# Odd layer: the next tile's projection between the score products and the probability turns of each attention block

## The reference

```python
def sliding_window_attention(h, w_qkv, q_gain, k_gain, sinks):
    qkv = jnp.einsum('bld,de->ble', h, w_qkv)        # 1024 -> 1024 q + 128 k + 128 v
    ...
    q = rms_norm(q, q_gain) * (HEAD_DIM ** -0.5)     # 16 query heads of 64
    k = rms_norm(k, k_gain)                          # 2 key heads
    ...
    s = jnp.einsum('bnqhgd,bnkhd->bhgnqk', qb, kw)   # 128 queries x (128 before + 128 own) keys
    ...
    s = s - slopes * dist.astype(f32)
    s = jnp.where(valid, s, -jnp.inf)
    m = jnp.maximum(jnp.max(s, axis=-1, keepdims=True), sink)
    p = jnp.exp(s - m)
    p = p / (jnp.sum(p, axis=-1, keepdims=True) + jnp.exp(sink - m))
    o = jnp.einsum('bhgnqk,bnkhd->bnqhgd', p, vw)
```

## Time and profile before

| | |
|---|---|
| median of 3 runs | 974.62 us (974.48 to 975.08) |
| profiled execution | 972.04 us |
| its span | 970.3 us, so 1.74 us lie around it |
| mean granted TensorE clock | 0.915 of full speed |
| busy in the span | PE 812.2 us, DVE 588.8, ACT 471.8, POOL 180.3 |

### The profile page before, as it was taken

How to read it: one execution, slowest core, us unless ns; L and a number is a source line. 1 busy time by engine, 2 the same in 40 slices (tenths; PEclk the granted TensorE clock), 3 DMA queues, 4 the chain that set the end, 5 groups by cost and what they waited for, 6 DMA issues and landing times. The chain is left out here.

```text
span 970.3 us, 10750 instructions
## 1 busy us (share of the span) xinstructions
PE 812.2 (84%) x4088; PEld 578.6 (60%) x4088; DVE 588.8 (61%) x782; ACT 471.8 (49%) x640; POOL 180.3 (19%) x175
## 2 busy tenths in 40 slices
PE   4999999757799489998973999477779939999894
PEld 3455454357488468887751555344448827888673
DVE  2898842097734669988750322766613457898882
ACT  6052002431623258887754100577742517887872
POOL 5300002230001214333220000311100212333311
PEclk9999999959899589999995999588889959999998
DMA  9212012100522859999983005200033376999972
GB/s 378 106 53 88 31 57 87 44 1 1 227 98 104 310 205 327 327 330 316 334 281 113 1 0 173 88 1 1 1 129 110 136 288 242 328 333 337 304 253 35
DMA packets 31161, 159.53 MB, mean 164 GB/s; under 512 B 7680, under 2 KB 7808, under 8 KB 15744
## 3 DMA queue, kind: packets, MB, share of 16 engines
q1 hardware_dynamic: 17856, 127.93, 35.5%
q0 software_dynamic: 11520, 25.20, 9.2%
q10 hardware_dynamic: 1728, 5.64, 1.5%
HBM read 150.34 MB, written 25.17 MB: 181 GB/s over the span
## 5 line engine op out<-in xcount | busy, mean ns | idle before, releaser
L840 DVE TENSOR_TENSOR w_lo<-ring,w_hi 128x2048 fp32r<-128x2048 f32 x93 | 211.6, 2288 | 55.3 <-ACT w_hi L605 30.1
L1781 PE MATMUL PS<-w_hi,left_hi 128*128 128x512 f32 x512 | 177.1, 408 | 8.7 <-DVE left_hi L840 8.5
L605 ACT ACTIVATE w_hi<-ring 128x2048 fp32r<-128x2048 f32 x86 | 164.0, 1914 | 22.5 <-DMA ring<-stream 21.8
L1781 PEld LDWEIGHTS PS<-w_hi,left_hi 128*128 128x128 f32 x512 | 97.8, 191 | 31.1 <-DVE left_hi L840 11.7
L1781 PE MATMUL PS<-w_lo,left_hi 128*128 128x512 f32 x256 | 101.2, 395 | 0.0
L1805 PE MATMUL PS<-w_hi,left_lo 128*128 128x512 f32 x256 | 84.8, 392 | 5.0 <-DVE left_lo L840 3.3
L1870 PE MATMUL PS<-ring,hT 128*128 128x512 f32 (+1 forms) x192 | 71.6, 533 | 0.8 <-DVE hT L840 0.8
L475 POOL DMA_INDIRECT arena<-rows x32 | 50.9, 1591 | 82.4 <-PE PS L1763 65.6
L1805 PEld LDWEIGHTS PS<-w_hi,left_lo 128*128 128x128 f32 x256 | 48.0, 188 | 17.1 <-DVE left_lo L840 3.7
L1870 PEld LDWEIGHTS PS<-ring,hT 128*128 128x128 f32 x192 | 37.0, 194 | 34.5 <-issue 31.9
L660 ACT ACTIVATE arena<-PS 128x512 f32<-128x512 f32 x16 | 9.5, 596 | 97.1 <-PE PS L1521 97.1
(11 more groups left out here) (259 smaller groups left out, 1381.9 us busy)
## 6 DMA issues: line engine op xcount, KB each, us to landing
ring<-stream SPq DMA_DIRECT2D x110, 1024.0 KB, 12.4
arena<-stream SPq DMA_DIRECT2D x6, 1024.0 KB, 8.5
rows<-arena POOLq DMA_DIRECT2D x8, 512.0 KB, 3.2
x<-stream SPq DMA_DIRECT2D x4, 1024.0 KB, 5.8
x<-x_in SPq DMA_DIRECT2D x4, 512.0 KB, 5.4
sums<-x POOLq DMA_DIRECT2D x4, 512.0 KB, 4.1
x<-sums ACTq DMA_DIRECT2D x4, 512.0 KB, 5.2
out<-x POOLq DMA_DIRECT2D x4, 512.0 KB, 4.1
```

What stands on the lines that cost most here:

```text
L605: act.activation(w_hi[pair], held_slot(layer, m), ACT.Copy).then_inc(w_hi_done, 1)
L840: return V.tensor_tensor(out, a, b, op)
L1781: ins = mm(PS[:, 2, :], a, b, start=k == 0 and t == 0, stop=k == KD - 1 and t == 2)
```

## The change

TensorE's order in this stretch becomes one loop over tiles. Projections 1 to 3 are cut into pieces: a projection function takes the part and the rows of products, and the pieces go between the steps of the previous tile's attention. Scores use banks 0 and 1 for both halves, all projections banks 2 to 4, the turns of heads and probabilities banks 5 and 6, the product with the values bank 7. The queries' heads have two buffers instead of four. ACT and DVE get queues in matching order: heads of tile tt + 1 after the maximum of the second block of tile tt on DVE; squares, roots and exponentials alternating on ACT; all copies of heads on DVE; the first weight split straight after the first tile's root. On DVE an odd block's first bias stands ahead of the sums of the block before. The instructions' number and shapes in projection, scores, turns and products stay as they are. The core of the diff, in the order ACT, DVE, TensorE:

```diff
-        qn = cut(xs_t, 0, TT, QW)
+        qn = [arena[:, 21504 + QW * i:21504 + QW * (i + 1)] for i in range(2)]
...
+            act.wait_ge(at_zero, 1)
+            squares(0)
+            head_deviation(0)
+            weights_hi(1, 0)
+            exps(0)
+            normed_odd(0)
+            for u in range(8):
+                tt = u // 2 + 1
+                if u % 2 == 0 and tt < TT:
+                    squares(tt)
+                turned_probs(u)
+                if u % 2 == 0 and tt < TT:
+                    head_deviation(tt)
+                if u < 7:
+                    exps(u + 1)
+                attended_hi(u)
+                if u < 7:
+                    normed_odd(u + 1)
...
+            def biased(u, t):
+
                 pr = probs[u % 2]
-                if u >= 2:
+                if u >= 2 and t == 0:
                     dve.wait_ge(pt_psum, 4 * (u - 1))
...
+                dve.wait_ge(s_psum, 2 * u + t + 1)
+                for j in (2 * t, 2 * t + 1):
+                    for kv in range(2):
+                        head = 8 * kv + 4 * (u % 2) + j
+                        ins = stt(pr[:, 2 * j + kv, :], table, con("slope")[:, head:head + 1],
+                                  PS[:, kv, (j % 2) * 256:(j % 2) * 256 + 256], ALU.mult, ALU.add)
+                ins.then_inc(s_biased, 1)
...
+            normed_heads(0)
             for u in range(8):
-                biased(u)
-                summed(u)
-                if u >= 1:
-                    attended(u - 1)
+                tt = u // 2
+                if u % 2 == 0:
+                    if u:
+                        summed(u - 1)
+                    heads_out(tt)
+                    if u:
+                        attended(u - 2)
+                    biased(u, 0)
+                else:
+                    biased(u, 0)
+                    summed(u - 1)
+                    if u >= 2:
+                        attended(u - 2)
+                biased(u, 1)
+                most(u)
+                if u % 2 and tt + 1 < TT:
+                    normed_heads(tt + 1)
+            summed(7)
+            attended(6)
             attended(7)
...
+            def project(tt, part, ks):
+
+                if part == 0 and 0 in ks:
+                    pe.wait_ge(hT_done, 2 * TT + 2 * tt + 2)
+                    if tt:
+                        pe.wait_ge(qkn_done, tt)
+                n = 512 if part < 2 else 256
...
+            def turn_heads(tt):
+
+                pe.wait_ge(qkn_done, tt + 1)
+                if tt:
+                    pe.wait_ge(pt_done, 4 * (2 * tt - 1))
...
+            def att_scores(u, t):
+
                 n, jq = u // 2, u % 2
...
+                if t == 0 and jq == 0:
+                    pe.wait_ge(qT_done, 3 * n + 3)
+                if u + t:
+                    pe.wait_ge(s_biased, 2 * u + t)
...
+            def attend(u):
+
                 n = u // 2
-                if u + 1 < 8:
-                    att_scores(u + 1)
+                if u % 2 and n + 1 < TT:
+                    pe.wait_ge(qT_done, 3 * n + 6)
...
+            whole, low, high = range(KD), range(4), range(4, KD)
+            for part in range(3):
+                project(0, part, whole)
+            for t in range(1, TT):
+                turn_tile(1, t)
+            pe.wait_ge(hT_done, 4 * TT)
+            for tt in range(TT):
+                more = tt + 1 < TT
+                if more:
+                    project(tt + 1, 0, low)
+                turn_heads(tt)
+                if tt:
+                    attend(2 * tt - 1)
+                att_scores(2 * tt, 0)
+                if more:
+                    project(tt + 1, 0, high)
+                att_scores(2 * tt, 1)
+                if more:
+                    project(tt + 1, 1, whole)
+                    project(tt + 1, 2, whole)
+                att_scores(2 * tt + 1, 0)
+                att_scores(2 * tt + 1, 1)
+                attend(2 * tt)
+            attend(7)
```

More of the change, by code:

```diff
@@ L314, in if_over @@
                 body(over[layer])
[L316 to L324, removed]
         def k512(i):
@@ L789, in _, with squares @@
             norm(2)
-            act.wait_ge(at_zero, 1)
-            for tt in range(TT):
+            def squares(tt):
                 act.wait_ge(qkv_psum, tt + 1)
@@ L795, in _, with head_deviation, exps @@
                     act.wait_ge(ss_a, tt)
[L796 to L800, removed]
+                act.activation(sq1, PS[:, 2:4, :].rearrange("p a b -> p (a b)"), ACT.Square)
+                act.activation(arena[:, 1024:1152], PS[:, 4, 0:128], ACT.Square).then_inc(sqa_done, 1)
+                act.activation(vpad[:, 1 + tt, 0, 0:64], PS[:, 4, 128:192], ACT.Copy)
+                act.activation(vpad[:, 1 + tt, 1, 64:128], PS[:, 4, 192:256], ACT.Copy)
+            def head_deviation(tt):
                 act.wait_ge(ss_a, tt + 1)
                 act.activation(qstd, qss, ACT.Sqrt, bias=eps_t, scale=1.0 / HD).then_inc(qstd_s, 1)
[L803 to L806, removed]
+            def exps(u):
                 pr = probs[u % 2]
@@ L1373, in _, with normed_heads @@
             ts(kq_gain, par("q_gain"), HD ** -0.5, ALU.mult)
-            for tt in range(TT):
-                if tt in (1, 2):
-                    heads_out(tt - 1, (0, 1, 0), V.tensor_copy, dve)
-                b = 2 + 3 * (tt % 2)
+            def normed_heads(tt):
                 dve.wait_ge(sqa_done, tt + 1)
@@ L1857, in _ @@
             turn_tile(1, 0)
-            def project(tt):
-                pe.wait_ge(hT_done, 2 * TT + 2 * tt + 2)
-                b = 2 + 3 * (tt % 2)
-                if tt >= 2:
-                    pe.wait_ge(qkn_done, tt - 1)
-                for part in range(3):
-                    n = 512 if part < 2 else 256
-                    for k in range(KD):
-                        if tt == 0 and (k == 0 or k == 4 and part < 2):
-                            full(QKV0 + 2 * part + k // 4)
-                        w = k512(QKV0 + 2 * part + k // 4)[:, k % 4, :] if part < 2 else \
-                            slot(QKV0 + 4).rearrange("p (k n) -> p k n", n=256)[:, k, :]
-                        ins = mm(PS[:, b + part, 0:n], hT[:, k, tt * 128:tt * 128 + 128], w, start=k == 0, stop=k == KD - 1)
-                        if tt == 3 and part < 2 and k % 4 == 3:
-                            ins.then_inc(slot_free, 1)
-                ins.then_inc(qkv_psum, 1)
@@ L1875, in turn_heads @@
-            def turn_heads(tt, banks):
-                pe.wait_ge(qkn_done, max(tt + 1, 4) if tt >= 2 else tt + 1)
+            def project(tt, part, ks):
[4 more added lines that the diff above has]
+                n = 512 if part < 2 else 256
+                for k in ks:
+                    if tt == 0 and (k == 0 or k == 4 and part < 2):
+                        full(QKV0 + 2 * part + k // 4)
+                    w = k512(QKV0 + 2 * part + k // 4)[:, k % 4, :] if part < 2 else \
+                        slot(QKV0 + 4).rearrange("p (k n) -> p k n", n=256)[:, k, :]
+                    ins = mm(PS[:, 2 + part, 0:n], hT[:, k, tt * 128:tt * 128 + 128], w, start=k == 0, stop=k == KD - 1)
+                    if tt == 3 and part < 2 and k % 4 == 3:
+                        ins.then_inc(slot_free, 1)
+                if part == 2:
+                    ins.then_inc(qkv_psum, 1)
+                    pending[0] = 1 if tt == 3 else 0
```

97 lines of the change are left out of this document (36 added, 61 removed).

## The result

The changed kernel takes **987.33 us** (986.07 to 989.11, 4 runs) against 974.55 us of the kernel before on the same chip (972.24 to 975.08): ratio 1.0137 with an interval of 1.0114 to 1.016, so 12.8 us slower. Forecast were 7.3 us, 981.9 in all: the right sign, and the size within the range (its end, 988, lies 0.7 us above the first median), but 4 to 5.5 us too small.

The account below looks back on a forecast made before the run. TensorE bounds the projections, a serial DVE and ACT chain each attention block (11.6 us). Cycles of 41.1 us against 41.98, plus exposed head and tail, put the output projection 7.3 us later: 974.62 + 7.3 = 981.9 us, range 977 to 988.

Parts of the forecast that it names:

- head: Before the first cycle: TensorE waits 10.4 us for the first tile's heads, starts at 561.3, loses 2.4 us to low clock.
- tail: Last tile's attention, with no projection to cover it: output projection starts at 727.4 instead of 720.11, 7.3 us later.
- step 4: In each cycle, half a projection part (3.44), four transposes (0.52), three DVE copies (1.5) and hand-overs (0.3): 5.75 us.
- step 6: In each cycle, three score halves of 1.0 us and the remaining projection pieces, 3.44 and 10.3: 16.75 us.
- Steps 1 to 3: DVE's serial chain from an odd block's first score half through biases, maximum and next tile's heads: 12.65 us.
- step 5: In each cycle, TensorE's turns and product of the odd block before the next scores: 5.93 us.
- a rival at 987: TensorE's clock falls in each cycle too, 1.7 to 3 us for each of two, more in the tail; chance 0.12.
- The table loads: ACT's square root and exponential switches, two loads a tile of 1.28 us each; the load before the root costs nothing.
- The rival of held loads: ACT's table loads are held behind the wait for the sums: 3.8 us more, 985.7 us; chance 0.07.
- No stall at the port: POOL's subtraction starts after DVE's last head product, making the start 4.3 us shorter: 977.6 us; chance 0.11.
- Faster, by a projection covered in full: Each cycle is TensorE's work alone, 34.5 us, saving 6.6 in each of two cycles: 968.7 us; chance 0.10.
- Transfers: Five QKV transfers of 4.8 us each, after their slots come free, stay hidden with nothing behind them until 727.

Follow-up runs that it names:

- the repetition: The changed kernel, with nothing altered, run and profiled once more in another series: 984.43 us against 973.07 for the kernel before, ratio 1.0131.

## Why the prediction was right, and where it was short

Its steps against the two traces, us. S is the end of the first score half of an odd block, 587.46 in the first trace (586.40 and 1.06 until the piece or the next work may start) and 586.34 in the repetition; the sum's times stand relative to the start of the stretch, which was 1.0 and 0.1 us later than before.

| | forecast | after | repetition |
|---|---|---|---|
| start of stretch to S (head) | 36.1 | 36.5 | 36.3 |
| cycle 1 | 41.1 | 43.5 | 42.05 |
| cycle 2 | 41.1 | 44.1 | 41.8 |
| S of block 5 to output projection | 59.1 | 62.4 | 60.8 |
| stretch | 177.4 | 186.4 | 181.0 |

The table also shows where the loss lies. Before, a tile took 41.98 us by the prediction's own reading, so two tiles 84.0 and the rest of the stretch 86.2. In the repetition the two cycles take 83.9 us, as much as before, and head and tail 97.1; in the first trace 87.5 and 98.9. So 10.9 to 12.7 us are lost in head and tail, which nothing covers (9.0 forecast), and 0 to 3.6 in the cycles, where a gain of 0.9 us each was forecast and none came.

- **Head: right to 0.4 us**, with two small errors against each other (step 4 came 0.3 us shorter than 2.4 + 5.6, step 6 0.6 longer). TensorE was forecast for 561.3, or 562.3 with the later start; it was 562.42, after 10.34 us. The stall of 4.58 us came again to the hundredth. The low clock cost 2.1 us (5.68 instead of 3.6 for the first piece), 2.4 assumed.
- **Steps 1 to 3: right.** Maximum at S + 7.8 (7.6 forecast), the heads' last product at S + 12.7 (12.65), wait of 2.48 (2.1). The claim that heads and biases come into one chain is what the traces show, and step 5, 5.93, was 5.92.
- **Step 6 was short by 0.6 in every cycle.** I divided 2.00 us for 16 score instructions by two and 17.19 for the projection by 40. Cut up, a score half takes 1.06 from its start to the next work, a half part 3.63 and three halves' worth 10.52: 3 x 1.06 + 3.63 + 10.52 = 17.33, not 16.75.
- **Step 4 is a term that failed, by its clock.** It has 3.44 us for the piece. The ground for full speed stands with the rivals: "A wait of 2.21 us before 239.01 left the clock at 1.00". From its start to the next work it took 5.2 in both cycles of the first trace (+1.8) and 3.5 in both of the repetition. Table of stages after, over the first 4 us of the piece:

```profile
600.29:604.29 4.00, 4.00 (x6) 1.70 (x7) 0.37 (x2) 3.97 (x14) 1.41 (x1) 0.57 0.00 0
614.66:618.66 4.00, 4.00 (x14) 1.78 (x14) 1.66 (x4) 0.00 (x0) 0.00 (x0) 1.00 0.00 0
```

  Rows 11 was one wait behind 5.6 us of work and ahead of more than 4. Here three follow one another from 586.40 to 600.29, 1.76, 1.20 and 2.48, with scores, turns and a product between them. I judged each wait singly. That the clock falls I had as a rival at 987 with a chance of 0.12. The traces show it in three of the four cycles: in both of the first trace, and in the first of the repetition, where it meets work with time to spare. In the fourth it stayed at 1.00 through the same waits. Of the two medians, 987.3 lies at that rival and 984.4 midway between it and the forecast. That 987.3 still lies within the stated range is owed to its upper end, which takes in this rival, and not to the forecast's own sum.
- **The table loads: as forecast in the first cycle, 0.3 to 0.5 late after.** The load ran before the wait:

```profile
595.03 1.28 ACT L794 ACT_TABLE_LOAD   x1
```

  and the root followed at 596.53, S + 9.07 (S + 9.0 forecast). In the second cycle the turns ran at the low clock (3.32 us from their start to the product, 2.59 in the repetition), the copies of the turns ended later, DVE waited 0.91 us for the root, and the piece started at S + 13.4; in the repetition's second cycle, at full clock, it started at S + 12.9. So the clock reaches the chain of DVE too, by way of ACT's copies, which no term of the prediction has. The rival of held loads (3.8 us) is refuted: in the head the load stands at 556.50 and its exponentials at 580.80. Of a second half of the price, a drain, no row shows anything: from the end of the root (596.84) to the next exponential (598.16) it is 1.32 us, of which the load is 1.28.
- **Tail: 1.7 to 3.3 short.** Two things. Three of the four score halves ran at the low clock, 2.08 us for 1.13, where I had put 1.0, and the last turns start 0.7 us late against S; and the last turns and product took 6.9 us in the repetition and 8.5 in the first trace (727.49 to 736.02) where I had put 5.93, though the same paragraph uses 8.0 for block 5, which took 6.85. PE of the first trace:

```profile
702.97 2.08 PE L1945 MATMUL PS<-arena 64*128 64x256 f32 x8 [1.82 <-DVE arena L861]
...
731.12 4.90 PE L1967 MATMUL PS<-arena 128*128 128x512 f32 x8
```

- **The other rivals.** No stall at the port: no, 4.58 us were there. Faster, by a projection covered in full: it needed DVE to do sums and heads without waiting for scores; the waits stood as listed, and the cycle of a quarter of the projection, 37.0 us, is longer than the 34.5 that this rival gave it, with three quarters of the work gone from TensorE. Transfers: nothing waited for them, as forecast.

What remains open: which executions meet the low clock and where, what the two missing score banks cost, and why the time outside the stretch varies by almost 5 us, which blurs every difference of medians of 2 us here.

## What to carry to other kernels

Before work of a free engine is put into the gaps of a chain, ask what the new order does to the chain: here the cover was real (12 to 17 us more of the projection hidden) and lost to what the new order cost: the next tile's heads and the waits for score banks came into the chain that DVE works through, which kept the cycles from gaining, and a head and a tail that nothing covers took 11 to 13 us. How much each single cause in the cycles costs was not measured. Where the blocks are bound by DVE and ACT in turn, running those two one block apart gives more (10 us of stretch against the same order with the same late split) than feeding TensorE. And judge TensorE's clock over a run of waits, not for each wait by itself.

## What the runs showed of the hardware that I had not expected

- The granted clock fell in a stretch in which TensorE was never idle for more than 1.8 us at once before the fall (with only the last wait filled: waits of 1.76 and 1.20, then a product that came 3.6 us after the turns instead of 2.6 and took 4.83 us instead of 3.60), while a single wait of 2.21 us had left it at 1.00, and while waits of 1.83, 1.20 and 2.47 us left it at 1.00 in the repetition's second cycle. With the waits filled by unneeded products it stayed at 1.00 from about 570 us to 688.
- Two executions of the same program on the same data showed the fall in different work, 5.37 or 3.67 us for the same piece; with it the stretch was 186.4 or 181.0 us.
- A row of projection products that score products follow takes about 0.2 us more from its start to the next work than its share of an unbroken row: 3.63 for 3.44, 10.52 for 10.32, besides 1.06 for 1.00 for a score half. Followed by the heads' turns, the same half part took 3.51.
